# A decode-and-prompt transformer layer: a new compression with a third fewer products per key block, the input norm moved into it, and stores and page loads moved across stage ends

## What is computed

```
idx = arange(nc)[:, None] * 16 + arange(32)[None, :]      # blocks of 32 tokens, one every 16
blk = rows[:, idx] + pos_emb                              # rows: (2048 tokens, 2 groups, 128)
hid = gelu(blk.reshape(..., 32 * 128) @ w1)               # w1: (4096, 128)
out = hid @ w2                                            # w2: (128, 128)
```

## Time and profile before

| | us |
|---|---|
| median of three executions (lowest, highest) | 2632.16 (2631.30, 2635.83) |
| the profiled execution's own time | 2622.21 |
| span from its first to its last instruction | 2620.2 |
| PE busy, all stages | 2160.3 |
| PE weight loads busy (beside PE) | 1339.8 |
| DVE, ACT, POOL busy | 441.0, 246.7, 108.0 |

### The profile page before, as it was taken

The page is one execution under the profiler, slowest core; times in us unless marked ns, Lnnn a source line. Parts: engine busy times, 40 slices in busy tenths (PEclk is TensorE's granted clock), DMA queues, the critical chain, the costliest instruction groups (busy, mean ns, idle before and its releaser), DMA issues. The chain is left out here.

```text
span 2620.2 us, 33664 instructions
## 1 busy us (share of the span) xinstructions
PE 2160.3 (82%) x13995; PEld 1339.8 (51%) x13995; DVE 441.0 (17%) x1052; ACT 246.7 (9%) x650; POOL 108.0 (4%) x124
## 2 busy tenths in 40 slices
PE   8999399999976999996877788899994577777773
PEld 7888267777756766664444344576332223322321
DVE  0000010002571121221112111111004111111112
ACT  0000110001210021211001000100001000000000
POOL 0000000000000000000000000000001111112211
PEclk9999699998985999998898988899996788888986
DMA  5552623332323332332999999843327899999998
GB/s 201 145 153 88 243 81 115 126 126 83 113 96 110 109 112 93 101 104 97 413 412 413 407 410 413 333 164 116 116 74 289 340 406 409 413 409 407 401 410 336
DMA packets 130950, 614.69 MB, mean 235 GB/s; under 512 B 29716, under 2 KB 34085, under 8 KB 93157
## 3 DMA queue, kind: packets, MB, share of 16 engines
q1 hardware_dynamic: 107166, 561.97, 55.4%
q0 software_dynamic: 22800, 45.07, 4.8%
q10 hardware_dynamic: 856, 5.77, 0.5%
HBM read 702.95 MB, written 39.60 MB: 283 GB/s over the span
## 5 line engine op out<-in xcount | busy, mean ns | idle before, releaser
L423 PE MATMUL bank<-ut,wring 128*128 128x320 f32 x1408 | 382.6, 433 | 0.0
L423 PEld LDWEIGHTS bank<-ut,wring 128*128 128x128 f32 x1408 | 267.3, 191 | 110.4 <-issue 1.3
L686 PE MATMUL bank<-ut,wring 128*128 128x320 f32 x1024 | 303.0, 442 | 16.9 <-ACT selmask L849 15.0
L686 PEld LDWEIGHTS bank<-ut,wring 128*128 128x128 f32 x1024 | 191.3, 193 | 93.5 <-issue 27.3
L1938 PE MATMUL bank<-wdn,par 128*32 128x512 f32 x512 | 91.3, 849 | 110.1 <-issue 108.9
L1380 PE MATMUL bank<-wring,arena 128*128 128x512 f32 x256 | 118.4, 605 | 3.1 <-DVE arena L1417 1.6
L1909 PE MATMUL bank<-wgu,arena 128*32 128x512 f32 x1024 | 118.4, 602 | 0.8 <-DVE arena L1989 0.8
L247 PE MATMUL bank<-arena,wring 128*128 128x256 f32 x512 | 115.9, 389 | 2.1 <-DMA arena<-in_cmp_kv 2.1
L558 DVE RECIPROCAL snew<-snew 128x320 f32<-128x320 f32 x30 | 64.5, 2149 | 314.0 <-ACT snew L527 314.0
L247 PE MATMUL bank<-zt,wring 128*128 128x256 f32 x512 | 111.8, 379 | 0.0
L247 PEld LDWEIGHTS bank<-arena,wring 128*128 128x128 f32 x512 | 99.9, 196 | 16.4 <-DMA arena<-in_cmp_kv 2.2
(11 more groups left out here) (394 smaller groups left out, 2077.7 us busy)
## 6 DMA issues: line engine op xcount, KB each, us to landing
wgu<-in_w_gu SPq DMA_DIRECT2D x128, 1024.0 KB, 17.0
wdn<-in_w_dn SPq DMA_DIRECT2D x32, 2048.0 KB, 25.1
wring<-in_w_proj SPq DMA_DIRECT2D x44, 1024.0 KB, 4.8
arena<-in_kv_k SPq DMA_DIRECT2D x64, 640.0 KB, 10.2
arena<-in_kv_v SPq DMA_DIRECT2D x64, 640.0 KB, 17.0
wring<-in_w_gate SPq DMA_DIRECT2D x32, 1024.0 KB, 5.1
wring<-in_w_merge SPq DMA_DIRECT2D x32, 1024.0 KB, 4.8
wring<-in_kv_k SPq DMA_DIRECT2D x32, 640.0 KB, 15.8
```

The lines of the kernel that those rows point to most:

```text
L423: last = nc.tensor.matmul(m.bank[:, 2 + s % 2, 0:T], m.wring[:, s, k * P:(k + 1) * P], m.ut[:, k, :], start=(k == 0), stop=(k == KD - 1))
L686: last = nc.tensor.matmul(m.bank[:, 6 + n % 2, 0:T], m.wring[:, n % 3, k * P:(k + 1) * P], m.ut[:, k, :], start=(k == 0), stop=(k == KD - 1))
```

## The change

**Compression.** Let E be the even and O the odd strides of 16 tokens (E(j) = stride 2j, O(j) = stride 2j+1). Blocks that begin at an even stride are w1a E(j) + w1b O(j), those that begin at an odd one w1a O(j) + w1b E(j+1). The new code forms (w1a + w1b) O(j) once and adds w1a (E(j) - O(j)) to it for the even ones, w1b (E(j+1) - O(j)) for the odd ones: three chains of 16 matmuls of 256 columns in place of four. A unit is now a pair of sequences and keys or values: 8 units of 48 matmuls. DVE forms the weight sums and, for each unit, the differences, one unit ahead of use; the second difference is written over the even rows. cmp_kv is laid out anew on the host: (page, keys or values, 128 partitions, 256), so a transfer is 128 KB with 1 KB a partition, 32 to a unit; SP issues those of one sequence, ACT those of the other.

**The norm.** x_t is loaded in the compression, the squares (ACT), the 16 matmuls of ones (PE), root, reciprocal and scaling are placed behind units 2 to 7, and the first two w_proj tiles are loaded behind the last keys' unit. In the projection only tiles 2 and 3, w_small and the cosines are loaded at the head; the w_small product stands behind the first four tiles.

**Stage ends.** The wait for the six stores moves into the prompt attention; the wait for the gate stores moves into the decode. The first four key pages of the decode are loaded by SP in the prompt attention, after the last gate weight tile was asked for; the decode's first load is then set 1, and blockof is loaded behind it. Slots 0 and 1 of the key ring change places in the arena.

```
+            for u in range(2, NU):
+                load(sp, u, 0)
+            sp.wait_ge(pre_done, NU - 1)
+            for s in range(2):
+                sp.dma_start(m.wring[:, s, :], a["w_proj"][s, :, :]).then_inc(m.w_in[s], 16)
...
+        def load(eng, u, e):
+            pair, kv = u // 2, u % 2
+            for pg in range(PAGES):
+                v = eng.value_load(m.pages[0:1, (2 * pair + e) * PAGES + pg:(2 * pair + e) * PAGES + pg + 1], min_val=0,
+                                   max_val=NPHYS - 1)
+                if pg == 0 and u >= 2:
+                    eng.wait_ge(pre_done, u - 1)
+                eng.dma_start(rows[u % 2][:, e * PAGES + pg, :, :, :].rearrange("p i e n -> p (i e n)"),
+                              a["cmp_kv"][bass.ds(v, 1), kv, :, :].rearrange("o p n -> (o p) n")
+                              ).then_inc(rows_in[u % 2], 16)
...
+            for u in range(NU):
+                kv, s = u % 2, u % 2
+                pe.wait_ge(w_sum_ready, kv + 1)
+                pe.wait_ge(rows_in[s], 512 * (u // 2 + 1))
+                if u >= 2:
+                    pe.wait_ge(sum_ready, u - 1)
+                chain(m.bank[:, s, 0:256], w_sum[kv], [rows[s][:, :, l, 1, :] for l in range(HALF)])
+                if u == 0:
+                    position(1)
+                if u >= 2:
+                    second(u - 2)
+                pe.wait_ge(diff_ready, 2 * u + 1)
+                chain(m.bank[:, 2 + s, 0:256], w1[kv][:, HALF:CBLK, :], [ahead[:, l, :, :] for l in range(HALF)]
+                      ).then_inc(ahead_read, 1)
+                pe.wait_ge(diff_ready, 2 * u + 2)
+                chain(m.bank[:, s, 256:512], w1[kv][:, 0:HALF, :], [rows[s][:, :, l, 0, :] for l in range(HALF)]
+                      ).then_inc(pre_done, 1)
+                if u - 1 in NORM_AT:
+                    r = NORM_AT[u - 1]
+                    pe.wait_ge(sqx_ready, r + 1)
+                    for k in range(4):
+                        last = nc.tensor.matmul(m.bank[:, 7, 0:T], m.c("ones"), sqx[r % 2][:, k, :],
+                                                start=(r == 0 and k == 0), stop=(r == 3 and k == 3))
+                    last.then_inc(norm_done, 1)
...
+            for u in range(NU):
+                if u + 2 < NU:
+                    load(act, u + 2, 1)
+                act.wait_ge(sum_ready, u + 1)
+                act.wait_ge(act_ready, 2)
+                nc.scalar.activation(hid[:, u % 2, :], hid[:, u % 2, :], ACT.Gelu_apprx_tanh,
+                                     bias=m.posc[:, u % 2:u % 2 + 1]).then_inc(act_ready, 1)
...
+                for g in range(G):
+                    nc.vector.tensor_tensor(out[:, :, :, g, 0:3], even[:, :, :, g, 1:4], odd[:, :, :, g, 0:3], ALU.subtract)
+                for e in range(2):
+                    c = slice(e * PAGES, e * PAGES + PAGES - 1)
+                    nxt = slice(e * PAGES + 1, e * PAGES + PAGES)
+                    last = nc.vector.tensor_tensor(out[:, c, :, :, 3], even[:, nxt, :, :, 0], odd[:, c, :, :, 3], ALU.subtract)
+                last.then_inc(diff_ready, 1)
+                dve.wait_ge(diff_ready, 2 * u + 1)
+                nc.vector.tensor_tensor(r[:, :, :, 0, :], r[:, :, :, 0, :], r[:, :, :, 1, :], ALU.subtract
+                                        ).then_inc(diff_ready, 1)
...
-            sp.wait_ge(m.stores, 6 * 16)
...
+            sp.wait_ge(pe_s, E_CMPO)
+            for i in range(4):
+                number = sp.value_load(m.pages[0:1, i:i + 1], min_val=0, max_val=NPHYS - 1)
+                sp.dma_start(m.ring[0][:, i, :], a["kv_k"][bass.ds(number, 1), :, :].rearrange("o p n -> (o p) n")
+                             ).then_inc(m.set_in[0], 16)
+            sp.wait_ge(m.stores, 6 * 16)
...
-            for s in range(2):
-                sp.wait_ge(g_out[s], 16 * KD)
...
-                for q in range(4):
+                for q in range(1 if isinstance(b, int) else 0, 4):
                     load_set("k", b * 8 + q, q, number)
+                    if isinstance(b, int) and q == 1:
+                        for s in range(2):
+                            sp.wait_ge(m.g_out[s], 16 * KD)
+                        at = C_AT["blockof"][0]
+                        sp.dma_start(m.blockof, a["consts"][0:NSB, at:at + PAGES * P]).then_inc(m.rows_in, 16)
```

More of the change, by code:

```diff
@@ L252, in second @@
-            def second(i, s, kv):
-                first = isinstance(i, int)
-                pe.wait_ge(hid_ready, i * 4 + (2 * s + kv + 1))
-                if not first:
-                    pe.wait_ge(out_kept, i * 4 + (2 * s + kv - 3))
-                if kv == 0:
-                    nc.tensor.matmul(m.bank[:, 4 + s, 0:G * NC_S], m.p("w2_k"), hid[:, kv, :],
-                                     start=True, stop=True).then_inc(out_done, 1)
-                else:
-                    for g in range(G):
-                        last = nc.tensor.matmul(m.bank[0:NC_S, 6 + s, g * P:(g + 1) * P],
-                                                hid[:, kv, g * NC_S:(g + 1) * NC_S], m.p("w2_v"), start=True, stop=True)
-                    last.then_inc(out_done, 1)
@@ new lines, in chain @@
+            def chain(out, w, src):
+                for l in range(HALF):
+                    last = nc.tensor.matmul(out, w[:, l, :], src[l], start=(l == 0), stop=(l == HALF - 1))
+                return last
+            position(0)
+            for u in range(NU):
[6 more added lines that the diff above has]
+                if u == 0:
+                    position(1)
+                if u >= 2:
+                    second(u - 2)
[12 more added lines that the diff above has]
+                    last.then_inc(norm_done, 1)
@@ new lines, in _ @@
+            nc.vector.memset(m.eps[:, :], EPS)
+            step(nc.vector.memset(ahead, 0.0))
+            weights(0)
+            for u in range(NU):
+                if u:
+                    sums(u - 1)
+                differences(u)
+                if u == 0:
+                    weights(1)
+                if u >= 2:
+                    keep(u - 2)
+                if u == 7:
+                    dve.wait_ge(rs_ready, 1)
+                    nc.vector.reciprocal(rs, rs).then_inc(rs_ready, 1)
+                    dve.wait_ge(rs_ready, 2)
+                    for k in range(KD):
+                        nc.vector.scalar_tensor_tensor(out=m.ut[:, k, :], in0=m.ut[:, k, :],
+                                                       scalar=m.p("norm_mix")[:, k:k + 1], in1=rs, op0=ALU.mult, op1=ALU.mult)
@@ L364, in _ @@
         def _(sp):
-            for c in range(4):
-                sp.dma_start(xt[:, 4 * c:4 * c + 4, :], a["x_t"][:, 4 * c:4 * c + 4, :]).then_inc(x_in, 16)
+            for s in range(2, SLOTS):
+                sp.dma_start(m.wring[:, s, :], a["w_proj"][s, :, :]).then_inc(m.w_in[s], 16)
             sp.dma_start(wsmall, a["w_small"].rearrange("p (k c) -> p k c", k=KD)).then_inc(csw_in, 16)
@@ L428, in _ @@
                 product(s, s)
+            pe.wait_ge(csw_in, 32)
+            for k in range(KD):
+                last = nc.tensor.matmul(m.bank[0:64, 1, 0:T], wsmall[:, k, :], m.ut[:, k, :],
+                                        start=(k == 0), stop=(k == KD - 1))
+            last.then_inc(small_done, 1)
             with pe.Fori(1, 7) as i:
```

234 lines of the change are left out of this document (105 added, 129 removed).

## The result

| | before | after |
|---|---|---|
| median of four executions each, us | 2633.99 (2631.3 to 2637.37) | 2514.9 (2511.19 to 2518.48) |
| the profiled execution's own time, us | 2622.21 | 2518.48 |
| its span, us | 2620.2 | 2516.7 |
| mean granted clock | 0.899 | 0.902 |

After over before is 0.9547, with an interval of 0.9524 to 0.957: 119.1 us less, where -120 was predicted (2512.0 against 2514.9). One word of the title is wrong: with three chains of products in place of four, a key block takes a quarter fewer products, not a third. The prediction's sums used 384 in place of 512.

The account below looks back on a forecast made before the run. Matmuls were taken to bound the compression and DMA bytes the decode, with TensorE mostly idle at the projection's head. Terms -45, +1, -62.7, +1, -6, -7.5 sum to -119.2, taken as -120: median 2512 us, range 2497 to 2540.

Parts of the forecast that it names:

- Part 1: Compression: 128 fewer matmuls save 55.4 us; with norm, loop breaks, tail and start the sum is -45, +1 in six units.
- VectorE's cover: Compression: new differences, about 12 of a 20.8 us unit, hide at cost 0; first-deadline margin 0.1 to 1.0 us.
- Rival (b): Compression: VectorE too slow, all differences at the strided price; +19 us, 2531; chance 7%.
- The loads' cover: Compression: a unit's row loads take 19.4 us within 21.6 if ScalarE issues as SP does; +1 at start, +1 in six units.
- D: Compression: time to issue and land a unit's row loads; 19.4 us expected, 27 at POOL's issue price.
- Rival (a): Compression: rows late through ScalarE's issue or 1 KB rows; up to +36 us, 2548; chance 17%.
- Part 2: Projection's head: only the small product of 71.3 us stays; net -62.7 us, and +1 for loads beside the window copy.
- Part 3: Projection's end: SP no longer waits for stores, so the gate gather moves earlier; -6 us, ends -3 and -8.
- Part 4: Decode's entry: stream starts 1.9 us earlier and carries four pages less, 6.5 us; -7.5, ends -1.9 and -8.4.
- Rival (d): Decode: the prefetch does not do what it says, blockof and page numbers hold the start; +6 us, 2518; chance 8%.
- (e): Compression: slower than before through ScalarE's queue, at 3.7 us per transfer issued; 2640 at 3.8; chance 2%.
- (f): Whole kernel: more gain, stores the full 8, decode 8.4, no loss in start or tail; -128 to -132, 2502; chance 8%.

Follow-up runs that it names:

- e0_after: The changed kernel run once more with no edit, for a second trace: 2510.02 us, ratio 0.9549 to the kernel before.
- e7: Changed kernel with the third chain of every unit run twice, so products are 512 as before: 2569.05 us, ratio 0.9766.
- e2: Changed kernel with two more unread VectorE differences ahead of each unit's first deadline: 2510.5 us, ratio 0.9547.
- e1: Changed kernel with SP issuing the compression's row loads of both sequences and ScalarE none: 2608.74 us, ratio 0.9911.
- e9: Changed kernel with the first two w_proj tiles loaded at the projection's head, not in the compression: 2526.28 us, ratio 0.9599.
- e8: Changed kernel with POOL's 8 MB window copy held until the first eight w_proj tiles' products are done: 2509.81 us, one execution.
- e3: Changed kernel with SP's wait for the six stores put back at the end of the projection: 2513.75 us, ratio 0.9564.
- e5: Changed kernel with the gate-store wait and blockof ahead of the decode's first keys, four pages still loaded ahead: 2512.01 us, ratio 0.9563.
- e4: As e5, but without the four key pages loaded ahead: 2511.97 us, one execution.
- e10: Changed kernel with blockof first, page numbers read early, and one-column matmuls spread among unit 0's last two chains: 2502.82 us, ratio 0.95.

## Why the prediction was right, by its steps

**Part 1, the compression's matmuls: -44 predicted, -43.9 measured in the result's own trace, and -48.7 with e0_after.** The -55.4 stands by e7. Between the first and the last sums copy the terms are 7 x 48 x 0.4325 = 145.3, the norm's 8.6 and six second layers of 1.02: 160.0, where the trace has 160.4. The tail was sized too long: from the last hidden product to the end of the last copy 4.7 us, not 7. The start was sized too short: +1 was written, and unit 0 ended at 64.0, some 5 us later than before's terms leave for it (273.0 less 221.4, 6.9, 3.3 and 3 leave 38.4; after, 64.0 less 20.8 is 43.2). In e0_after it ended at 60.0, +0.8. So that term scatters between the two. That -44 and -43.9 agree is partly luck: two misses of opposite sign, in a trace with a long start. PE's share, forecast at 0.95 or more, was 0.93 in both traces: PE stood idle for 16.9 us of before's compression, and still does for 16.6 of the shorter one. The stage's last copy ended at 229.1, where 228 had been said.

**VectorE's cover.** The prices held: 1.71 to 1.75 us for 1536 against 1.75, 1.0 for a page edge, as the strided row had given, and 4.43 for 4096. The Trainium skill (SBUF — State Buffer, "Door 1: The DMA port swizzle") would have runs of three floats within a line at full rate and the page edges slow; the trace agrees, with 1.1 ns a float in the runs and 2.1 in the edges. Rival (b), all at the strided price, is out. Its mechanism was tested by e2; the margin of 0.1 to 1.0 was right for unit 1 (0.2) and low for units 4 to 7, where I didn't count the norm's matmuls as slack.

**The loads' cover.** ScalarE issues a transfer in 1.04 us, SP in 1.07, and 1 KB rows landed in 2.8 us (median), so D was 19.6 against the 19.4 taken. Rival (a) is out, and e1 shows what it would have cost. The fear of 1 KB rows came from a line drawn through 2 KB and 5 KB rows at different loads; a unit needs 4.2 MB in 21 us, some 200 GB/s, and the issue spreads them that thin.

**Part 2, the head: -61.7 predicted, -60.2 measured** (-60.4 between the second traces). No run puts the norm back into the projection; that the removed wait is what was gained is read from the head's rows, PE busy 22 of 71 us before and 45.3 of 45.3 after, and e9 tests the early tiles alone. The tiles landed before they were wanted, as the step said, though in another pattern: 6.0 and 27.0 us where 10 and 25 were worked out from x_t's rate. From the turn-taking between queues that the Trainium skill states (DMA: Bandwidth & Descriptors, "Queues, rings and completion order"), the prediction drew a growing margin. The traces neither bear it out nor refute it: tile 2 landed 4 us earlier than by the row, tile 3 after 18.3 to 27.6 us where the row gave 25, so the margin at the tight place was 9 us in e0_after and 0.7 in the result's trace. The cost through the copy was 0 (e8), where +1 had been taken. What is missing is the clock: the four first products took 36.6 and not 34.6 us, all of it in the first product, whose first 4 us had a granted clock of 0.50 to 0.67. The prediction had 1.00 there. The stretch from the compression's end to the fifth w_proj product was 46 us, under the 50 that would have counted against it.

**Part 3, the stores: -6 predicted, -5.2 to -6.0 measured** (5.0 to 5.5 by e3). It lay where the step put it, in the gather's issue.

**Part 4, the decode: -7.5 predicted, -6.1 to -7.3 measured, by the pair of traces.** Part of it was mis-sized. The step "at most 1 lost", for blockof behind set 1, was 1.4 to 2.0 in the stream of page loads (after and e0_after against e5); the stream's gain was 4.4 to 5.1 us, where 6.5 less at most 1 was taken. The start of the stream gave 2.4 where 1.9 was taken. The prediction looked for the loss in late scores and a stream that runs dry; what the traces show is a stream that never stopped and carried blockof slowly for 3 us. Rival (d), that the prefetch does nothing, is out by e4.

**The sum to a median.** The profiled execution was to take about 2502 us and took 2518.5: that step failed by 16 us. The sum came out right because it was taken from the median as well. The first trace of before was fast by itself, in the prompt stretch and behind the decode, where the second stood 8.4 and 5.8 us longer, and nothing carried that over to the kernel after, whose profiled execution lay 3.6 us above its median.

**Rivals (e) and (f).** For (e) ScalarE would have needed 3.7 us an issue and took 1.04. For (f) the stores and the decode would have had to reach 8 and 8.4 us, and did not.

## What to carry over

When products are replaced by sums and differences on another engine, the products' time comes back in full only while the covers hold (the issue of the loads, the adder's first deadline, what is loaded for the next stage); work each out as slack in us, since here they were 0.2 to 2 us wide in most places (0.7 to 9 for the tile behind the copy), and in e1, e2 and e9 what went beyond them was lost nearly one for one. At a stage bound by a stream, look at what the issuing engine does between its last wait and the stream's first transfer: 16 register reads there were worth 8 us, more than four prefetched pages. Before a stretch of some hundred us is explained by one trace, take a second trace of the same kernel.

## What was not expected of the hardware

**Two executions of one program differ in the granted clock.** The start of the compression in after and in e0_after, same code, columns as in the table by stretch:
```profile
36.00:48.00 12.00, 12.00 (x67) 11.90 (x67) 2.49 (x2) 1.63 (x3) 0.00 (x0) 0.62 1.02 333
```
```profile
32.00:44.00 12.00, 12.00 (x80) 11.45 (x78) 6.45 (x2) 1.45 (x2) 0.00 (x0) 0.86 1.02 319
```
The block of one-column matmuls ran in 11.35 and 9.03 us, and the 16 products behind it in 9.59 and 8.67, where the next 16 took 7.07. That is 3.2 of the 4.0 us between the two starts. The other 0.8 lies in the 16 products ahead of the block (9.75 and 8.98 us), at a granted clock of 1.00 in both, and is not explained. e10 shows that the block has to do with the clock: with its matmuls spread among the products the clock stayed at 1.00, and unit 0 ended earlier than in any other run. In the prompt stretch, lengths near 413 and near 421 us turn up in both kernels, with some between; the clocks over it are 0.93 to 0.95, and I did not find what chooses among them.

**A copy of 8 MB beside loads of 1 MB** delays the second load from 8 us to between 18 and 28, and not the first: the tile asked for first lands in 5.4 to 6.1 us with the copy and 6.0 without it.

**Scores 17 us earlier were worth nothing.** That is how far they moved between e0_after and e5, with the decode's length unchanged at 448.3 us: the stream began 1.5 us later and was 1.4 shorter, and the DMA engines' share was 1.01 to 1.02 along the stream in both.
